# A seven-product feed-forward projection over ten of sixteen chunks of K instead of eight

## The chip, the cores and the metric

The kernel runs on one core of one Trainium2 chip. The metric is the device time of one execution in microseconds; before the change it is 1642.07 us, the median of three runs (1641.97 to 1642.49). All data are float32.

## What is computed

Two transformer blocks run one behind the other on 256 tokens of width 2048: a mixer block (attention, short convolution, pooling, output projection, layer norm), and a block of gated linear attention, a SwiGLU feed-forward part, a gate with an embedding and a last norm. The change touches the feed-forward part alone:

```python
def swiglu(hn, w_in, w_out):            # hn (256, 2048), w_in (2048, 11264), w_out (5632, 2048)
    gate, up = jnp.split(jnp.einsum('btd,de->bte', hn, w_in), 2, axis=-1)
    return jnp.einsum('btf,fd->btd', jax.nn.silu(gate) * up, w_out)
```

## The kernel before

**Products in split float32.** Every float32 operand is split in two: a rounded high part (`hi`, type float32r, by a ScalarE copy) and the rest (`lo = x - hi`, by a VectorE subtraction). A product is then three matmuls: hi x hi, hi x lo, lo x hi. So a block of weights with K rows in chunks of 128 costs one ScalarE copy, one VectorE subtraction and three matmuls for each chunk and each of the two tiles of 128 tokens.

**The feed-forward loop.** The inner width 5632 is cut into `NF = 11` steps of 512 columns. In step f the kernel computes the 512 gate and the 512 up columns (K = 2048, 16 chunks), and the part of the output product that belongs to step f-1 (`o0` to `o3`, four blocks of 4 chunks by 512 columns, each for both token tiles).

**Seven products for eight.** Chunks 8 to 15 are multiplied plainly: `g0` and `g1` (gate), `u0` and `u1` (up), four chunks each for both token tiles, 24 matmuls a block. Chunks 0 to 7 are taken as a two-by-two block product in the Strassen-Winograd form. The blocks on the one side are the token tile (first or second 128) by the half of the chunks (0 to 3 or 4 to 7); on the other side the half of the chunks by gate or up (`w11`, `w12`, `w21`, `w22`). Eight block products become seven, `f11 f21 f22 ft1 ft2 ft3 ft4`, each for one token tile of sums, 12 matmuls. The sums on the side of the weights are made in each step by VectorE in place (`block_sum`, line 2157, four a step), those on the side of the activations once (`form_sums`, `s_hi`, `s_lo`). VectorE combines the seven results (`combine`, line 2164, eight 128x512 operations a step).

**The order of the work.** It is written out by hand, and each engine takes its own list in order. On TensorE a step is

`g0 f11 g1 (turn) f21 u0 ft1 o0 f22 u1 ft2 o1 ft3 o2 ft4 o3`

where `turn` transposes the activations of step f-1 (line 1066). ScalarE makes the `hi` of the same blocks in the same order (lines 1499 and 1511), with `copy_p1` (1518, which takes the result of `f11` out of the accumulator), the `silu` calls (1525) and `split_act` (1585, of the transposed activations, between `ft1` and `o0`) among them. VectorE makes the `lo` (2144) in the same order; between the `lo` of `ft1` and of `o0` stand the low half of `split_act` (2275, two operations) and one `block_sum`.

**Buffers.** There are `SPLITS = 3` pairs of `hi` and `lo` buffers used in turn, so the `hi` of a block waits until TensorE is done with the block three places before it. There are `RAWS = 6` buffers for raw weights. SyncE issues the loads (line 576) in order, each as soon as the `lo` that used the buffer last is done: `w11` and `w21` follow the `lo` of `ft4` of the step before, `g1` the `lo` of `o3`.

**The first and the last step.** The first step (`FIRST`) has no output blocks and takes `g0 u0 f11 g1 ft1 f21 f22 ft2 ft3 ft4 u1`. The last (`LAST`) takes `ft3 ft4 o1 o2 o3` at its end. Ahead of the first stands the last panel of the projection before, which reads its operand from `y_hi` and `y_lo`.

Of the kernel before, what the change touches and what calls it, by code (L numbers as in the profile page):

```python
# [76 lines left out]
RAWS, SPLITS = 6, 3  # L77
FORMS = 7
# [26 lines left out]
(L_X, L_Y, L_Z, L_22A, L_22, L_21, L_11, L_12) = range(1, COMBOS + 1)  # L105
EARLY_0 = 6
# [149 lines left out]
def block_kernel(nc, x, x_cols, w_in, fg_cols, b_f, columns, pool_cols, w_out, ln_g, ln_b, p_cols,  # L256
# [7 lines left out]
    def at(name, shape, dt, offset):  # L264
# [73 lines left out]
    s_sum = [at(f"s_sum{k}", [P, QUAD, P], F32, W + (40 + 2 * k) * KB) for k in range(4)]
    s_hi = [at(f"s_hi{k}", [P, QUAD, P], F32R, s_at[k]) for k in range(FORMS)]
    s_lo = [at(f"s_lo{k}", [P, QUAD, P], F32R, s_at[FORMS + k]) for k in range(FORMS)]  # L340
    up = [at(f"up{t}", [P, N], F32, (108 + 2 * t) * KB) for t in range(TT)]
    act_tok = at("act_tok", [P, TT, N], F32, 80 * KB)
    act_hi = at("act_hi", [P, N // P, TOK], F32R, 84 * KB)
    act_lo = at("act_lo", [P, N // P, TOK], F32R, 88 * KB)
# [58 lines left out]
    with ExitStack() as ctx:  # L403
# [109 lines left out]
        def s_sources():  # L513
# [3 lines left out]
            return ((F11, h_cols[:, 0:QUAD, one]), (F21, h_cols[:, QUAD:, one]), (FT4, h_cols[:, QUAD:, two]),  # L517
# [8 lines left out]
        def _(sp):  # L526
# [35 lines left out]
            def quad_rows(w, r, col):  # L562

                return w[r:r + QUAD * P, col:col + N].rearrange("(c p) n -> p c n", p=P)

            def load_quad(key, src):

                slot, count, freed = RAW[key]
                place = (slot + 2) % RAWS
                if freed is not None:  # L570
                    sp.wait_ge(d_lo_done, freed + 1)
                elif place < 2:
                    sp.wait_ge(lo_done, U_END - RING + 2 * (place + 1))
                else:
                    sp.wait_ge(unit_used, U_END - RING + 2 * (place % 2 + 1))
                sp.dma_start(d_raw[slot][:], src).then_inc(d_landed[slot], 16)

            def load_in(name, f, row, col):

                load_quad((name, f), quad_rows(ffn_w_in[0], row * QUAD * P, col * D_FF + f * N))  # L580

            def load_out(name, f, n):

                load_quad((name, f), quad_rows(ffn_w_out[0], (f - 1) * N, n * N))

            load_in("g0", 0, 2, 0)
            load_in("u0", 0, 2, 1)
            load_in("w11", 0, 0, 0)
            load_in("w12", 0, 0, 1)
            load_in("g1", 0, 3, 0)  # L590
            load_in("w22", 0, 1, 1)
            load_in("w21", 0, 1, 0)
            load_in("u1", 0, 3, 1)
            for f in range(1, NF):
                load_in("g0", f, 2, 0)
                load_in("w11", f, 0, 0)
                load_in("w21", f, 1, 0)
                load_in("g1", f, 3, 0)
                load_in("w12", f, 0, 1)
                load_in("u0", f, 2, 1)  # L600
                load_in("w22", f, 1, 1)
                load_out("o0", f, 0)
                load_in("u1", f, 3, 1)
# [123 lines left out]
        def _(pe):  # L727
# [305 lines left out]
            def quad_tile(e, bank, hi, lo, k, t, st, en):  # L1033

                tok = slice(t * P, (t + 1) * P)
                for c in range(QUAD):
# [3 lines left out]
                    mm = pe.matmul(bank[:], lo[:, k + c, tok], wh, start=False, stop=en and c == QUAD - 1)  # L1040
# [4 lines left out]
            def quad(e, banks, hi, lo, k, st, en, i=0):  # L1045

                pe.wait_ge(d_lo_done, i * E_STEP + (e + 1))
                for t in range(TT):
                    mm = quad_tile(e, banks[t], hi, lo, k, t, st, t in en)
# [25 lines left out]
            quad(FIRST["g0"], gate_banks, a_hi, a_lo, 2 * QUAD, True, NONE)  # L1075
# [4 lines left out]
            quad(FIRST["u0"], up_banks, a_hi, a_lo, 2 * QUAD, True, NONE)  # L1080
# [3 lines left out]
            quad(FIRST["g1"], gate_banks, a_hi, a_lo, 3 * QUAD, False, NONE)  # L1084
# [7 lines left out]
            quad(FIRST["u1"], up_banks, a_hi, a_lo, 3 * QUAD, False, BOTH)  # L1092
# [10 lines left out]
            def ffn_step(at, f, i=0, first=False, last=False):  # L1103

                pe.wait_ge(combined, EARLY_0 if first else i * COMBOS + COMBOS * f)
                quad(at["g0"], gate_banks, a_hi, a_lo, 2 * QUAD, True, NONE, i)
# [12 lines left out]
                quad(at["u1"], up_banks, a_hi, a_lo, 3 * QUAD, False, BOTH, i)  # L1119
# [71 lines left out]
        def _(act):  # L1191
# [301 lines left out]
            def high_of(e, raw, i=0):  # L1493
# [5 lines left out]
                nc.scalar.copy(d_hi[e % SPLITS][:], d_raw[slot][:]).then_inc(d_hi_done, 1)  # L1499

            def quad_high(at, name, f, i=0):

                high_of(at[name], (FORM_RAW.get(name, name), f), i)
# [24 lines left out]
            def split_h(name, n, col):  # L1528
                for i in (2 * n, 2 * n + 1):
                    split_high(name, i, a_hi, 2 * i, h1_hi_done if name == "h1" else h2_hi_done, col + 2 * i)  # L1530

            def columns_of(i, bank, done):

                for k in range(2):
                    c = 2 * i + k
                    last = nc.scalar.activation(h_cols[:, c, :], bank[:, k * TOK:(k + 1) * TOK], ACT.Copy,
                                                scale=vec[:, V_FFN + c:V_FFN + c + 1])
                last.then_inc(done, 1)

            for n in range(PO):  # L1540
                for j in range(UPP):
# [7 lines left out]
                    if n >= 1 and j == 1:  # L1549
                        if n == PO - 1:  # L1550
                            split_h("h1", n - 1, V_FFN)
                        else:
                            for i in (2 * n - 2, 2 * n - 1):
                                job_done(act, "h1", i)
                                columns_of(i, bank_of("h1", i), read_of("h1", i))
                        squares(1, n - 1)
                    if (n, j) == (2, 4):
                        act.wait_ge(s_summed, 4)
                        for k, src in s_sources():
                            nc.scalar.copy(s_hi[k][:], src).then_inc(s_hi_done, 1)  # L1560
# [26 lines left out]
            def ffn_step(at, f, i=0, last=False):  # L1587
# [76 lines left out]
        def _(dve):  # L1664
# [471 lines left out]
            def split_h(name, n, col):  # L2136
                for i in (2 * n, 2 * n + 1):
                    done, count = (h1_hi_done, 2 * (i - 3)) if name == "h1" else (h2_hi_done, 2 * (i + 1))
                    split_low(name, i, a_hi, a_lo, 2 * i, done, count, col + 2 * i)

            def low_of(e, slot, i=0):

                dve.wait_ge(d_hi_done, i * E_STEP + (e + 1))
                nc.vector.tensor_tensor(d_lo[e % SPLITS][:], d_raw[slot][:], d_hi[e % SPLITS][:],  # L2144
                                        ALU.subtract).then_inc(d_lo_done, 1)

            def quad_low(at, name, f, i=0):

                low_of(at[name], RAW[(FORM_RAW.get(name, name), f)][0], i)
# [275 lines left out]
```

## Time and profile before

| | |
|---|---|
| median of three runs | 1642.07 us |
| the profiled execution | 1642.43 us |
| its span, first to last instruction | 1640.7 us |
| TensorE busy | 1625.9 us, 99% |
| VectorE busy | 1224.6 us, 75% |
| ScalarE busy | 852.5 us, 52% |
| mean granted TensorE clock | 0.998 |
| DMA | 316.00 MB, 193 GB/s |

The feed-forward steps lie between 838 and 1519 us of the span. A matmul's record is longer than its share of the engine, since matmuls overlap: the distance from one start to the next is what it costs. The same holds in a smaller measure for VectorE and ScalarE, where the next instruction starts up to 0.1 us before the end of the record in front of it.

### The profile page before, as it was taken

How to read it: one execution, taken by the hardware profiler on the slowest of the kernel's cores; microseconds unless marked ns; L12 is line 12 of the kernel's file. 1: busy time of each engine (PE TensorE's matmuls, PEld its weight loads, DVE VectorE, ACT ScalarE, POOL GpSimd, SP SyncE). 2: the span in 40 equal slices, each digit the busy share in tenths (PEclk: the TensorE clock that was granted, in tenths of full speed). 3: DMA queues.
4: the chain of work that ended last, by engine and by line, in shares of the span. 5: the costliest groups of instructions: out<-in, count | busy, mean ns of one | idle time of the engine just before them, and what ended most of it. 6: DMA issues, size and time to landing. Idle time of an engine off the chain costs nothing.

```text
span 1640.7 us, 21707 instructions
## 1 busy us (share of the span) xinstructions
PE 1625.9 (99%) x8508; PEld 1337.3 (82%) x8508; DVE 1224.6 (75%) x1168; ACT 852.5 (52%) x880; POOL 57.1 (3%) x83
## 2 busy tenths in 40 slices
PE   9999999999999999999999999999999999999997
PEld 7888888888888888888887888888888888887886
DVE  5544476566787999765679988988888888889754
ACT  5435454444568565665555545454545554554543
POOL 7000000000010000000000000000000000000001
PEclk9999999999999999999999999999999999999999
DMA  8666655766575656635575546456467376365841
GB/s 278 174 186 184 189 162 160 232 226 211 164 246 165 187 173 180 181 116 189 163 250 205 185 174 242 164 207 231 138 221 255 109 249 226 132 230 213 299 154 52
DMA packets 156776, 316.00 MB, mean 193 GB/s; under 512 B 7360, under 2 KB 7360, under 8 KB 155808
## 3 DMA queue, kind: packets, MB, share of 16 engines
q1 hardware_dynamic: 155088, 304.12, 56.8%
q0 software_dynamic: 1616, 10.87, 1.8%
q8 instruction: 51, 0.84, 0.2%
q14 instruction: 21, 0.17, 0.0%
HBM read 310.77 MB, written 4.19 MB: 192 GB/s over the span
## 4 chain that ended last, share of the span: by engine, by line
PE 96%; DVE 2%; issue 1%; ACT 1%; POOLq 0%; POOL 0%; DVEq 0%; ACTq 0%
PE acc L739 15%; PE acc L741 15%; PE acc L740 15%; PE acc L1038 9%; PE acc L1039 9%; PE acc L1040 9%; PE aux L1038 7%; PE aux L1040 6%; PE aux L1039 6%; DVE d_lo L2144 1%; PE aux L755 1%; PE aux L925 1%; PE aux L767 1%; PE acc L1066 0%; PE aux L776 0%
## 5 line engine op out<-in xcount | busy, mean ns | idle before, releaser
L2144 DVE TENSOR_TENSOR d_lo<-d_raw,d_hi 128x2048 fp32r<-128x2048 f32 x181 | 413.8, 2287 | 117.2 <-ACT d_hi L1499 83.9
L1676 DVE TENSOR_TENSOR w_lo<-w_raw,w_hi 128x1024 fp32r<-128x1024 f32 x276 | 336.1, 1224 | 204.7 <-ACT w_hi L1198 203.9
L1198 ACT CAST w_hi<-w_raw 128x1024 fp32r<-128x1024 f32 x276 | 289.2, 1049 | 338.9 <-PE acc L741 309.9
L1499 ACT CAST d_hi<-d_raw 128x2048 fp32r<-128x2048 f32 x137 | 262.2, 1914 | 226.0 <-PE acc L1040 126.1
L739 PE MATMUL acc<-w_hi,a_hi 128*128 128x512 f32 x832 | 330.4, 397 | 0.0
L741 PE MATMUL acc<-w_hi,a_lo 128*128 128x512 f32 x832 | 324.2, 390 | 0.0
L740 PE MATMUL acc<-w_lo,a_hi 128*128 128x512 f32 x832 | 324.1, 390 | 0.0
L741 PEld LDWEIGHTS acc<-w_hi,a_lo 128*128 128x128 f32 x832 | 156.2, 188 | 33.1
L739 PEld LDWEIGHTS acc<-w_hi,a_hi 128*128 128x128 f32 x832 | 156.2, 188 | 32.0 <-issue 0.3
L740 PEld LDWEIGHTS acc<-w_lo,a_hi 128*128 128x128 f32 x832 | 156.4, 188 | 30.6
L1511 ACT CAST d_hi<-d_raw 128x2048 fp32r<-128x2048 f32 x44 | 84.2, 1914 | 116.6 <-PE aux L1040 67.5
L1038 PE MATMUL aux<-d_hi,a_hi 128*128 128x512 f32 x352 | 137.1, 390 | 0.7 <-DVE d_lo L2144 0.7
L1040 PE MATMUL aux<-d_hi,a_lo 128*128 128x512 f32 x352 | 136.9, 389 | 0.0
L1039 PE MATMUL aux<-d_lo,a_hi 128*128 128x512 f32 x352 | 136.9, 389 | 0.0
L1038 PE MATMUL acc<-d_hi,act_hi 128*128 128x512 f32 x320 | 124.8, 390 | 1.5 <-DVE act_tok L2191 1.5
L1040 PE MATMUL acc<-d_hi,act_lo 128*128 128x512 f32 x320 | 124.5, 389 | 0.0
L1039 PE MATMUL acc<-d_lo,act_hi 128*128 128x512 f32 x320 | 124.5, 389 | 0.0
L2157 DVE TENSOR_TENSOR d_raw<-d_raw,d_raw 128x2048 f32<-128x2048 f32 x44 | 100.4, 2283 | 1.0 <-DMA d_raw<-in_ffn_w_in 1.0
L739 PE MATMUL acc<-w_hi,y_hi 128*128 128x512 f32 x256 | 100.1, 391 | 0.0
L741 PE MATMUL acc<-w_hi,y_lo 128*128 128x512 f32 x256 | 99.7, 389 | 0.0
L740 PE MATMUL acc<-w_lo,y_hi 128*128 128x512 f32 x256 | 99.6, 389 | 0.0
L1038 PEld LDWEIGHTS aux<-d_hi,a_hi 128*128 128x128 f32 x352 | 66.1, 188 | 14.7 <-DVE d_lo L2144 1.1
(312 smaller groups left out, 2208.7 us busy)
## 6 DMA issues: line engine op xcount, KB each, us to landing
d_raw<-in_ffn_w_in SPq DMA_DIRECT2D x88, 1024.0 KB, 7.3
w_raw<-in_w_in SPq DMA_DIRECT2D x112, 512.0 KB, 3.7
w_raw<-in_gla_w_in SPq DMA_DIRECT2D x96, 512.0 KB, 3.8
d_raw<-in_ffn_w_out SPq DMA_DIRECT2D x44, 1024.0 KB, 5.1
w_raw<-in_w_out SPq DMA_DIRECT2D x32, 512.0 KB, 4.7
w_raw<-in_gla_w_out SPq DMA_DIRECT2D x32, 512.0 KB, 3.8
d_raw<-in_ple_w_gate SPq DMA_DIRECT2D x16, 1024.0 KB, 5.2
x_raw<-in_x_cols SPq DMA_DIRECT2D x8, 256.0 KB, 6.7
```

The source lines that it names most:

```text
L739: pe.matmul(banks[t][:], hi[:, k + c, tok], wh, start=st, stop=False)
L740: pe.matmul(banks[t][:], hi[:, k + c, tok], wl, start=False, stop=False)
L741: mm = pe.matmul(banks[t][:], lo[:, k + c, tok], wh, start=False, stop=en)
L1038: pe.matmul(bank[:], hi[:, k + c, tok], wh, start=st and c == 0, stop=False)
L1039: pe.matmul(bank[:], hi[:, k + c, tok], wl, start=False, stop=False)
L1040: mm = pe.matmul(bank[:], lo[:, k + c, tok], wh, start=False, stop=en and c == QUAD - 1)
L1198: nc.scalar.copy(w_hi[u % RING][:], w_raw[u % RING][:]).then_inc(hi_done, 1)
L1499: nc.scalar.copy(d_hi[e % SPLITS][:], d_raw[slot][:]).then_inc(d_hi_done, 1)
L1511: nc.scalar.copy(d_hi[e % SPLITS][:], d_raw[slot][:]).then_inc(d_hi_done, 1)
L1676: nc.vector.tensor_tensor(w_lo[u % RING][:], w_raw[u % RING][:], w_hi[u % RING][:], ALU.subtract).then_inc(lo_done, 1)
L2144: nc.vector.tensor_tensor(d_lo[e % SPLITS][:], d_raw[slot][:], d_hi[e % SPLITS][:], ALU.subtract).then_inc(d_lo_done, 1)
L2157: nc.vector.tensor_tensor(x[:], x[:], d_raw[SLOT[other]][:], ALU.add).then_inc(d_summed, 1)
```

## The change

The block products take ten chunks (`HALF = 5`, so two halves of five) and the plain blocks six: `g0` and `u0` have two chunks, `g1` and `u1` four. The output blocks keep four. With larger blocks the memory is laid out anew: the third pair of splits takes the place of `y_hi` and `y_lo`, so the first `f11` waits for the end of the panel before; `p1` and `cx` have no tiles of their own and lie in `act_tok`, `cy` lies in `up[1]`. `copy_p1` therefore waits until the old `act_tok` is turned, and stands behind the `hi` of `u0`. The split of the activation sums moves from the third to the fourth panel of the projection before. The loads of the end take the raw buffers in another order.

```diff
+HALF = 5
+PLAIN = (2, 4)
-(L_X, L_Y, L_Z, L_22A, L_22, L_21, L_11, L_12) = range(1, COMBOS + 1)
-EARLY_0 = 6
+(L_X, L_Y, L_12, L_Z, L_22A, L_22, L_21, L_11) = range(1, COMBOS + 1)
+EARLY_0 = 5
+def chunks_of(name):
+    if name in ("g0", "u0", "g1", "u1"):
+        return PLAIN[int(name[1])]
+    return HALF if name[0] in "fw" else QUAD
...
-        place(("fe", n), (1, 3, 0, 2)[n], E_FE + n)
+        place(("fe", n), (1, 3, 2, 4)[n], E_FE + n)
-        place(("pg", q), (4, 5, 1, 3, 0, 2)[q % RAWS], E_PG + q)
+        place(("pg", q), (5, 1, 3, 2, 4)[q % 5], E_PG + q)
...
-    d_raw = [at(f"d_raw{r}", [P, QUAD, N], F32, 8 * ((r + 2) % RAWS) * KB) for r in range(RAWS)]
-    d_hi = [at(f"d_hi{r}", [P, QUAD, N], F32R, W + 8 * r * KB) for r in range(SPLITS)]
-    d_lo = [at(f"d_lo{r}", [P, QUAD, N], F32R, W + (24 + 8 * r) * KB) for r in range(SPLITS)]
+    raw_at = [60 * KB, 16 * KB, 26 * KB, 36 * KB, 0, 8 * KB]
+    d_raw = [at(f"d_raw{r}", [P, HALF if r < 4 else QUAD, N], F32, raw_at[r]) for r in range(RAWS)]
+    d_hi = [at(f"d_hi{r}", [P, HALF, N], F32R, (W + 10 * r * KB, 80 * KB)[r == 2]) for r in range(SPLITS)]
+    d_lo = [at(f"d_lo{r}", [P, HALF, N], F32R, (W + (20 + 10 * r) * KB, 90 * KB)[r == 2]) for r in range(SPLITS)]
...
-    p1 = at("p1", [P, N], F32, W + 60 * KB)
-    cx = at("cx", [P, N], F32, W + 62 * KB)
-    cy = at("cy", [P, N], F32, W + 64 * KB)
+    p1, cx, cy = act_tok[:, 0, :], act_tok[:, 1, :], up[1]
...
-            quad(FIRST["g0"], gate_banks, a_hi, a_lo, 2 * QUAD, True, NONE)
+            quad(FIRST["g0"], gate_banks, g_hi, g_lo, 0, True, NONE, n=PLAIN[0])
...
-                mm = quad_tile(e, bank, s_hi[k], s_lo[k], 0, 0, st, en)
+                mm = quad_tile(e, bank, s_hi[k], s_lo[k], 0, 0, st, en, HALF)
...
-                nc.scalar.copy(d_hi[e % SPLITS][:], d_raw[slot][:]).then_inc(d_hi_done, 1)
+                nc.scalar.copy(d_hi[e % SPLITS][:, 0:n, :], d_raw[slot][:, 0:n, :]).then_inc(d_hi_done, 1)
...
                 act.wait_ge(d_used, i * E_STEP + (at["f11"] + 1))
                 if f:
-                    act.wait_ge(combined, i * COMBOS + (COMBOS * (f - 1) + C_11))
-                nc.scalar.copy(p1[:], acc[2][:]).then_inc(p1_read, 1)
+                    act.wait_ge(act_turned, i * TT + TT * f)
+                nc.scalar.copy(p1, acc[2][:]).then_inc(p1_read, 1)
...
-                    if (n, j) == (2, 4):
+                    if (n, j) == (3, 3):
                         act.wait_ge(s_summed, 4)
...
+            act.wait_ge(unit_used, U_END)
             act.wait_ge(s_lo_done, FORMS)
             quad_high(FIRST, "f11", 0)
...
                 quad_high(at, "g1", f, i)
                 quad_high(at, "f21", f, i)
+                quad_high(at, "u0", f, i)
                 copy_p1(at, f, i)
-                quad_high(at, "u0", f, i)
                 sum_high(at, "ft1", f, i)
                 split_act(f - 1, act_hi, acc[0:2], i)
...
                     quad_low(at, "o1", f)
-                    combine(cx[:], acc[0], cx[:], ALU.add, at["ft3"], f, 0, L_Y)
+                    combine(up[0][:], aux[2], cy[:], ALU.add, at["u1"], f, 0, L_Y)
+                    combine(cx, acc[0], cx, ALU.add, at["ft3"], f, 0, L_X)
...
                     combine(act_tok[:, 0, :], aux[0], p1[:], ALU.add, at["f21"], f)
-                    combine(up[0][:], aux[2], cy[:], ALU.add, at["u1"], f, 0, L_Y)
                     multiply(1, f)
```

## Rows read from the trace of the kernel before

**Rows 1.** The page, busy time: engine, us, share of span, instructions.
```profile
PE 1625.9 (99%) x8508; PEld 1337.3 (82%) x8508; DVE 1224.6 (75%) x1168; ACT 852.5 (52%) x880; POOL 57.1 (3%) x83
```
**Rows 2.** Waits of TensorE: released by, us in total, times, longest us.
```profile
PE acc L1038 <- DVE act_tok L2191: 1.5, 1, 1.5
...
PE acc L1038 <- DVE d_lo L2144: 0.8, 1, 0.8
PE aux L1038 <- DVE d_lo L2144: 0.7, 1, 0.7
```
**Rows 3.** Busy time by stretch: PE, PEld, DVE, ACT, POOL, clock, DMA share, GB/s.
```profile
1200.00:1260.00 60.00, 60.00 (x278) 49.49 (x277) 52.45 (x38) 30.46 (x20) 0.00 (x0) 1.00 0.54 185
1500.00:1560.00 60.00, 58.50 (x287) 48.11 (x286) 45.97 (x53) 32.41 (x46) 1.84 (x3) 1.00 0.85 316
1631.00:1641.00 10.00, 0.31 (x2) 0.00 (x0) 3.36 (x7) 2.56 (x4) 0.55 (x1) 0.70 0.55 210
```
**Rows 4.** Timeline of TensorE, one middle step: start, duration, first matmuls of blocks.
```profile
1021.69 0.39 PE L1040 MATMUL aux<-d_hi,a_lo 128*128 128x512 f32 x1
1022.01 0.71 PE L1066 MATMUL acc<-ident,act_tok 64*128 64x64 f32 x16
1022.66 0.50 PE L1038 MATMUL aux<-d_hi,s_hi 128*128 128x512 f32 x1
...
1025.53 0.39 PE L1038 MATMUL aux<-d_hi,a_hi 128*128 128x512 f32 x1
...
1030.97 0.39 PE L1038 MATMUL acc<-d_hi,s_hi 128*128 128x512 f32 x1
...
1033.69 0.39 PE L1038 MATMUL acc<-d_hi,act_hi 128*128 128x512 f32 x1
```
**Rows 5.** Timeline of ScalarE, same step.
```profile
1008.52 1.91 ACT L1499 CAST d_hi<-d_raw 128x2048 fp32r<-128x2048 f32 x1 [2.54 <-PE acc L1040]
...
1016.75 0.59 ACT L1518 COPY p<-acc 128x512 f32<-128x512 f32 x1 [0.88 <-PE acc L1040]
1017.24 1.91 ACT L1499 CAST d_hi<-d_raw 128x2048 fp32r<-128x2048 f32 x1
1022.12 1.91 ACT L1511 CAST d_hi<-d_raw 128x2048 fp32r<-128x2048 f32 x1 [2.97 <-PE aux L1040]
```
**Rows 6.** Timeline of VectorE, same step.
```profile
1024.06 2.29 DVE L2144 TENSOR_TENSOR d_lo<-d_raw,d_hi 128x2048 fp32r<-128x2048 f32 x1 [1.47 <-ACT d_hi L1511]
1026.27 1.28 DVE L2275 TENSOR_TENSOR act_lo<-acc,act_hi 128x512 fp32r<-128x512 f32 x2
1027.47 2.28 DVE L2157 TENSOR_TENSOR d_raw<-d_raw,d_raw 128x2048 f32<-128x2048 f32 x1
1029.67 2.29 DVE L2144 TENSOR_TENSOR d_lo<-d_raw,d_hi 128x2048 fp32r<-128x2048 f32 x1
```
**Rows 7.** The page's groups: VectorE and ScalarE instructions of two and four chunks.
```profile
L2144 DVE TENSOR_TENSOR d_lo<-d_raw,d_hi 128x2048 fp32r<-128x2048 f32 x181 | 413.8, 2287 | 117.2 <-ACT d_hi L1499 83.9
L1676 DVE TENSOR_TENSOR w_lo<-w_raw,w_hi 128x1024 fp32r<-128x1024 f32 x276 | 336.1, 1224 | 204.7 <-ACT w_hi L1198 203.9
L1198 ACT CAST w_hi<-w_raw 128x1024 fp32r<-128x1024 f32 x276 | 289.2, 1049 | 338.9 <-PE acc L741 309.9
L1499 ACT CAST d_hi<-d_raw 128x2048 fp32r<-128x2048 f32 x137 | 262.2, 1914 | 226.0 <-PE acc L1040 126.1
```
**Rows 8.** Timeline of SyncE's DMA issues, same step.
```profile
996.47 0.92 SPq L576 DMA_DIRECT2D d_raw<-in_ffn_w_in  x2
...
1000.59 0.92 SPq L576 DMA_DIRECT2D d_raw<-in_ffn_w_in  x2
```
**Rows 9.** The tile of raw weights, window 1000 to 1002: `g1` and `w12`.
```profile
DMA to landing us min/median/max: 7.5/9.4/11.4
```
**Rows 10.** Timeline of TensorE: first matmuls of `g0` and `u1`, first step.
```profile
837.75 0.39 PE L1038 MATMUL aux<-d_hi,a_hi 128*128 128x512 f32 x1
...
875.87 0.50 PE L1038 MATMUL aux<-d_hi,a_hi 128*128 128x512 f32 x1 [0.66 <-DVE d_lo L2144]
```

More of the change, by code:

```diff
@@ L338, in block_kernel @@
[L338 to L344, printed above, removed]
@@ new lines, in block_kernel @@
+    s_hi = [at(f"s_hi{k}", [P, HALF, P], F32R, s_at[k]) for k in range(FORMS)]
+    s_lo = [at(f"s_lo{k}", [P, HALF, P], F32R, s_at[FORMS + k]) for k in range(FORMS)]
+    g_hi = at("g_hi", [P, KD - 2 * HALF, TOK], F32R, 48 * KB)
+    g_lo = at("g_lo", [P, KD - 2 * HALF, TOK], F32R, 54 * KB)
+    up = [at("up0", [P, N], F32, W + 67 * KB), at("up1", [P, N], F32, 46 * KB)]
+    act_tok = at("act_tok", [P, TT, N], F32, 100 * KB)
+    act_hi = at("act_hi", [P, N // P, TOK], F32R, 104 * KB)
+    act_lo = at("act_lo", [P, N // P, TOK], F32R, 108 * KB)
@@ L516, in s_sources @@
             one, two = slice(0, P), slice(P, TOK)
-            return ((F11, h_cols[:, 0:QUAD, one]), (F21, h_cols[:, QUAD:, one]), (FT4, h_cols[:, QUAD:, two]),
+            return ((F11, h_cols[0][:, :, one]), (F21, h_cols[1][:, :, one]), (FT4, h_cols[1][:, :, two]),
                     (FT1, s_sum[0][:]), (FT3, s_sum[2][:]), (FT2, s_sum[1][:]), (F22, s_sum[3][:]))
@@ L582, in load_out @@
-            def load_out(name, f, n):
[L584 to L593, printed above, removed]
-            for f in range(1, NF):
[L595 to L601, printed above, removed]
+                else:
+                    sp.wait_ge(*after)
@@ new lines, in _ @@
+            load_in("g0", 0, (lo_done, U_END - RING + 2))
+            load_in("u0", 0, (lo_done, U_END))
+            load_in("w11", 0, (unit_used, U_GO))
+            load_in("w12", 0, (unit_used, U_END - 1))
+            load_in("g1", 0)
+            load_in("w22", 0, (unit_used, U_END))
+            load_in("w21", 0, (unit_used, U_END))
+            load_in("u1", 0)
+            for f in range(1, NF):
+                load_in("g0", f)
+                load_in("w11", f)
+                load_in("w21", f)
+                load_in("g1", f)
+                load_in("w12", f)
+                load_in("u0", f)
+                load_in("w22", f)
@@ L1031, in _, with quad_tile @@
                         turn_h("h1", 2 * n - 1)
-            def quad_tile(e, bank, hi, lo, k, t, st, en):
+            def quad_tile(e, bank, hi, lo, k, t, st, en, n=QUAD):
                 tok = slice(t * P, (t + 1) * P)
-                for c in range(QUAD):
+                for c in range(n):
                     wh, wl = d_hi[e % SPLITS][:, c, :], d_lo[e % SPLITS][:, c, :]
@@ L1039, in quad_tile, with quad @@
                     pe.matmul(bank[:], hi[:, k + c, tok], wl, start=False, stop=False)
-                    mm = pe.matmul(bank[:], lo[:, k + c, tok], wh, start=False, stop=en and c == QUAD - 1)
+                    mm = pe.matmul(bank[:], lo[:, k + c, tok], wh, start=False, stop=en and c == n - 1)
                 return mm
             BOTH, NONE = range(TT), ()
-            def quad(e, banks, hi, lo, k, st, en, i=0):
+            def quad(e, banks, hi, lo, k, st, en, i=0, n=QUAD):
                 pe.wait_ge(d_lo_done, i * E_STEP + (e + 1))
                 for t in range(TT):
-                    mm = quad_tile(e, banks[t], hi, lo, k, t, st, t in en)
+                    mm = quad_tile(e, banks[t], hi, lo, k, t, st, t in en, n)
                 mm.then_inc(d_used, 1)
@@ L1491, in _, with high_of @@
                         stage_panel(P_G + p, og[p - 8], rstd[1], ACT.Silu)
[L1493 removed]
+            def high_of(e, raw, i=0, n=QUAD):
                 slot, count, _ = RAW[raw]
@@ L1529, in split_h, with columns_of, plain_columns @@
                 for i in (2 * n, 2 * n + 1):
[L1530 to L1532 removed]
+                    split_high(name, i, a_hi, 2 * i, h2_hi_done, col + 2 * i)
+            def columns_of(i):
+                job_done(act, "h1", i)
                 for k in range(2):
                     c = 2 * i + k
[L1536 to L1538 removed]
+                    last = nc.scalar.activation(h_cols[c // HALF][:, c % HALF, :], bank_of("h1", i)[:, k * TOK:(k + 1) * TOK],
+                                                ACT.Copy, scale=vec[:, V_FFN + c:V_FFN + c + 1])
+                last.then_inc(read_of("h1", i), 1)
+            def plain_columns():
+                i = HALF
+                job_done(act, "h1", i)
+                for k in range(2):
+                    c = 2 * i + k
+                    nc.scalar.activation(g_hi[:, k, :], bank_of("h1", i)[:, k * TOK:(k + 1) * TOK], ACT.Copy,
+                                         scale=vec[:, V_FFN + c:V_FFN + c + 1]).then_inc(h1_hi_done, 1)
             for n in range(PO):
@@ L1566, in _ @@
                     col = 2 * (2 * PO - 2 + k) + c
-                    last = nc.scalar.activation(a_hi[:, col, :], acc[k][:, c * TOK:(c + 1) * TOK], ACT.Copy,
+                    last = nc.scalar.activation(g_hi[:, col - 2 * HALF, :], acc[k][:, c * TOK:(c + 1) * TOK], ACT.Copy,
                                                 scale=vec[:, V_FFN + col:V_FFN + col + 1])
@@ L2168, in combine_xy @@
                 dve.wait_ge(p1_read, i + (f + 1))
-                combine(cx[:], acc[2], p1[:], ALU.subtract, at["ft2"], f, i)
-                combine(cy[:], acc[3], cx[:], ALU.add, at["ft1"], f, i, C_X)
+                combine(cx, acc[2], p1, ALU.subtract, at["ft2"], f, i)
+                combine(cy[:], acc[3], cx, ALU.add, at["ft1"], f, i, C_X)
             def combine_one(at, f, i=0):
                 dve.wait_ge(act_turned, i * TT + TT * f)
-                combine(act_tok[:, 0, :], aux[0], p1[:], ALU.add, at["f21"], f, i)
+                combine(act_tok[:, 0, :], aux[0], p1, ALU.add, at["f21"], f, i)
                 combine(up[0][:], aux[2], cy[:], ALU.add, at["u1"], f, i, C_Y)
             def combine_late(at, f, i=0):
-                combine(cx[:], acc[2], cx[:], ALU.add, at["ft3"], f, i, C_Y)
+                combine(cx, acc[2], cx, ALU.add, at["ft3"], f, i, C_Y)
                 combine(up[1][:], acc[2], cy[:], ALU.add, at["ft3"], f, i)
@@ L2195, in split_h @@
                 for i in (2 * n, 2 * n + 1):
-                    done, count = (h1_hi_done, 2 * (i - 3)) if name == "h1" else (h2_hi_done, 2 * (i + 1))
-                    split_low(name, i, a_hi, a_lo, 2 * i, done, count, col + 2 * i)
+                    split_low(name, i, a_hi, a_lo, 2 * i, h2_hi_done, 2 * (i + 1), col + 2 * i)
             def form_sums():
                 one, two = slice(0, P), slice(P, TOK)
-                a11, a12 = h_cols[:, 0:QUAD, one], h_cols[:, QUAD:, one]
-                a21, a22 = h_cols[:, 0:QUAD, two], h_cols[:, QUAD:, two]
-                for i in range(4):
+                a11, a12 = h_cols[0][:, :, one], h_cols[1][:, :, one]
+                a21, a22 = h_cols[0][:, :, two], h_cols[1][:, :, two]
+                for i in range(HALF):
                     job_read(dve, "h1", i)
@@ L2257, in _ @@
             dve.wait_ge(p1_read, 1)
-            combine(cx[:], acc[2], p1[:], ALU.subtract, FIRST["ft2"], 0)
-            combine(cy[:], acc[3], cx[:], ALU.add, FIRST["ft1"], 0, 0, C_X)
-            combine(act_tok[:, 0, :], aux[0], p1[:], ALU.add, FIRST["f21"], 0)
+            combine(cx, acc[2], p1, ALU.subtract, FIRST["ft2"], 0)
+            combine(cy[:], acc[3], cx, ALU.add, FIRST["ft1"], 0, 0, C_X)
+            combine(act_tok[:, 0, :], aux[0], p1, ALU.add, FIRST["f21"], 0)
             quad_low(FIRST, "u1", 0)
-            combine(cx[:], acc[0], cx[:], ALU.add, FIRST["ft3"], 0, 0, 3)
-            combine(up[1][:], acc[0], cy[:], ALU.add, FIRST["ft3"], 0)
+            combine(cx, acc[0], cx, ALU.add, FIRST["ft3"], 0, 0, 3)
             def combine_first_up():
                 combine(up[0][:], aux[2], cy[:], ALU.add, FIRST["u1"], 0)
-                combine(up[1][:], aux[3], up[1][:], ALU.add, FIRST["u1"], 0, 0, 5)
-                dve.wait_ge(combined, 7)
+                combine(up[1][:], acc[0], cy[:], ALU.add, FIRST["ft3"], 0)
+                combine(up[1][:], aux[3], up[1][:], ALU.add, FIRST["u1"], 0, 0, 7)
                 multiply(0, 0)
```

91 lines of the change are left out of this document (44 added, 47 removed).

## The prediction

> **What bounds the kernel now.** I read the busy times first: TensorE 99% of the span, VectorE 75%, ScalarE 52% [rows 1]. The whole kernel waits on TensorE's list. The waits of TensorE say the same: in the eleven feed-forward steps there are three, 1.5, 0.8 and 0.7 us [rows 2], two in the first step and one in the last. The stretches then show how near the next engine is: in 60 us of the middle steps TensorE is busy for 60.0 and VectorE for 52.45 [rows 3]. So a step has some 7.5 us of VectorE's time to spare in 60. That is an average. What decides is each place where a block's `lo` must be ready, and the places differ, so I looked at one step by engine [rows 4 to 6].
>
> **What a step costs each engine.** Twelve matmuls of `ft1` take from 1030.97 to 1033.69, so one costs 2.72 / 12 = 0.2267 us [rows 4]. Before, a step has 4 x 24 (plain) + 7 x 12 (products) + 4 x 24 (output) = 276. After: `g0` and `u0` 12 each, `g1` and `u1` 24 each, 7 x 15, 96: 273. TensorE saves 3 x 0.2267 = 0.68 us a step, 7.5 us in eleven steps. That is all that the change can gain.
>
> VectorE pays for it. Two chunks take 1224 ns and four 2287, so a chunk is 0.53 us and a five-chunk subtraction 2.82 (estimate by the straight line of these two rows) [rows 7]; the block sums are 2.28 and so 2.81 [rows 6]. A step gets 7 + 4 chunks more and 4 fewer: 7 x 0.53 = 3.7 us more on an engine that had some 7.5 to spare. ScalarE: 1049 and 1914 ns give 0.43 a chunk and 2.35 for five [rows 7]; it gets 3 chunks more, 1.3 us, and has half its time free. On the average both still fit under TensorE. The bytes of a step are the same: 16 chunks for gate, 16 for up, 16 for the outputs.
>
> **The place where it does not fit: `o0` in every step.** In the order of the work `u0` stands between the turn and `o0`, and it is one of the blocks that shrink. Before, from the last matmul of `g1` the chain is: `hi` of `ft1` at 1022.12, as soon as `g1` has left its buffers; `lo` of `ft1` at 1024.06; two `act_lo` at 1026.27; a block sum at 1027.47; `lo` of `o0` 1029.67 to 1031.96 [rows 5, 6]. TensorE comes to `o0` at 1033.69 [rows 4], so 1.73 us are left over.
>
> After, counted from the same `g1`:
> - TensorE. The turn and `f21` take from 1021.92 (0.23 behind 1021.69) to 1025.53 with 12 matmuls [rows 4]; with 15 `f21` ends at 1026.21. `u0` with 12 takes 2.72, to 1028.93; `ft1` with 15 takes 3.40, to 1032.33. `o0` is due 1.36 us earlier than before.
> - ScalarE. `copy_p1` stood at 1016.75 in the shadow of `g1` [rows 5]. It now writes into `act_tok`, so it waits for the end of the turn, 1022.01 + 0.71 = 1022.72, and what is queued behind it is the `hi` of `ft1`, `split_act`, `o0`. A waiting engine starts 0.04 after its releaser (1022.08 to 1022.12 [rows 4, 5]): 1022.76. The next instruction starts 0.49 later (1016.75 to 1017.24 [rows 5]): `hi` of `ft1` at 1023.25, 1.13 later than before, and ready at 1025.60.
> - VectorE. `lo` of `ft1` starts at 1025.63 and holds the engine for 2.21 + 0.53 = 2.74 (to 1028.37); `act_lo` 1.20 (1029.57); the block sum 2.20 + 0.53 = 2.73 (1032.30); `lo` of `o0` 2.29, ready at 1034.59 [steps from rows 6, 7].
>
> So data are 2.63 us later (1.13 by the wait for the turn, 0.43 and twice 0.53 by fifth chunks) and the need is 1.36 earlier; the 1.73 to spare turn into a stall of 2.30 with 0.04 for the release. The first matmul after a stop is 0.11 longer (0.50 against 0.39 [rows 10, 4]). A step: 2.30 + 0.11 - 0.68 = 1.73 us slower. No row shows a five-chunk instruction. From below, were the fifth chunk free (2.29 and 1.91), the data would come 1.49 earlier: a stall of 0.8, a step 0.25 slower. From above, in proportion with the fixed part (2.287 x 1.25 = 2.86, 1.914 x 1.25 = 2.39), 0.12 later: 1.85. The straight line through two and four chunks is the nearest, so I take 1.73.
>
> **`g1` and its load.** `w11` and `w21` are issued when the `lo` of `ft4` is done, 996.47, `g1` at 1000.59 [rows 8]; `g1` landed 7.5 us later [rows 9], so 11.6 after the first, with 3 MB in the queue. The queue moves up to 316 GB/s [rows 3], 3.3 us for 1 MB. In front of `g1` now stand 2.5 MB instead of 2: 13.25 us. ScalarE could start it at 1008.52 [rows 5], 12.05 after the issue; I take 12.45 after the change, as `ft4` is longer on TensorE. It waits 0.8. TensorE comes to `g1` 2.72 + 3.40 = 6.12 after that point, and `hi` 1.91, `lo` 2.2 and the multiply 0.74 (with the releases) need 4.95. So 0.35 is left. Landings of neighbouring loads scatter by about 1 us (7.5 and 11.4 for two issued together [rows 9]); I allow 0.2 a step, 1.8 for nine steps.
>
> **The first step.** It has no output blocks, so its 7 products and 4 sums crowd VectorE, which already stopped TensorE for 0.8 and 0.7 [rows 2]. The `hi` of `f11` now waits for the end of the panel, just past 837.75 [rows 10]: 837.95. Then `hi` to 840.30; VectorE: `lo` of `f11` to 843.07, sum to 845.80, the last columns of h (1.6) to 847.4, `lo` of `g1` to 849.6, a root (0.45) to 850.05, nine five-chunk instructions (5 `lo` and 3 sums up to `ft3`, and `ft4`) of 2.735 to 874.7, three combinations of 0.6 to 876.5, `lo` of `u1` (2.29) to 878.8. With some 0.3 of waits between, `u1` starts on TensorE at 879.1 against 875.87 [rows 10]: 3.2 slower. The moved split of the sums lies in the fourth panel, on VectorE and ScalarE, which have waits there; it ends about 2 us before `g0` is due: nothing.
>
> **The second step.** `ft4`'s `lo` ends near 874.8 and with it the loads start: `g1` lands at 888.1, is split at 892.3 and multiplied at 893.0; TensorE is there at 879.1 + 5.44 + 2.72 + 3.40 = 890.7. A stall of 2.3 and 0.1 for the start, and the 1.73 of `o0`: 4.1 slower.
>
> **The last step.** Its `o0` stalls like the others, +1.73. The stop of 1.5 at `o2` [rows 2] shrinks: one combination (0.6) has moved ahead of the `lo` of `o2`, and TensorE comes later. I take 0.7 off: +1.0. Behind it the raw buffers are five instead of six; a block of the end is 24 matmuls, 5.44 us, against 3.3 to load 1 MB: nothing. If that cover fell, each of 20 blocks could lose up to a microsecond.
>
> **Sum.** 3.2 + 4.1 + 8 x 1.73 + 1.0 + 1.8 = 23.9 us. The profiled execution took 1642.4 (span 1640.7 and 1.7 around it), 0.4 above the median of the runs: 1642.4 + 23.9 = 1666.3. As a second stall at `ft1` or `f22` costs more than a saved one gives back, I round up to 1667.
>
> **Rivals.**
> - *The loads decide.* For: `g1` has 0.35 us left, and 1.25 MB loads are longer. Against: bytes and the share of DMA time, 0.54 [rows 3], are unchanged. At 3.6 us for 1 MB `g1` lands 1.05 later; 0.7 to 1.1 a step, ten steps, 7 to 11 more: 1674 to 1678.
> - *TensorE stays the bound (the other side).* The stall at `o0` does not come, because VectorE and ScalarE run through that chain in the time that they have on the average. Then 11 x 0.68 = 7.5 less: 1635. For: 7.5 us to spare on VectorE in 60 against 3.7 [rows 3]. Against: the order of the lists; VectorE is idle while ScalarE waits for the turn and can't work ahead. It decides from a chain 1.7 us shorter, where stall and saving are equal.
> - *TensorE's clock falls.* The granted clock is 1.00 in the stretch with the stop of 1.5 us and 0.70 in the last 10 us, where TensorE is busy for 0.31 [rows 3]: between 1.2 and 2.4 GHz, 0.70 is 6 of 10 us at the lower. If each of some 14 stops of 2.3 us brought 3 us at half speed, 1.5 each: 21 more, 1688. The Trainium skill, page "TensorE: Matmul & The Clock Gate", section "HAM oscillation — how this bites in real kernels", says that waits repeated in a loop can make the clock fall and rise in each round. By that rule this rival holds; for it speaks that stops come in every step, against it that each is short and 57 us of dense work follow.
>
> **Chances.** The sum as worked out, 0.78 (1655 to 1672); loads 0.13; clock 0.04; faster 0.05. Times within 0.2% (3.3 us), about what a measurement of this kernel can tell from no change, need the stall near 0.7: I give 0.02, taken from the first and the faster case, so faster 0.04, slower 0.94. The range 1657 to 1679 leaves out the faster and the clock case and the ends of the others.
>
> **What would show it.** The waits of TensorE after: one group at `acc` released by `d_lo`, about ten times of 2.3 us, at `o0`; in ScalarE's row of the `p` copy a releaser of line 1066's turn; five-chunk rows 128x2560 of 2.8 us on VectorE and 2.35 on ScalarE. A wait at `g1` of 2 to 3 us in the second step alone. Step length 65.2; before it is 276 x 0.2267 and 0.89 for the turn (1021.92 to 1025.53 less 2.72) [rows 4], 63.5. Wrong, if the waits of TensorE are under 7 us in all, if they stand at other blocks than `o0`, or if the clock is below 0.99.

## The result, and the profile after

The changed kernel takes 1670.61 us (median of six runs, 1669.84 to 1671.34) against 1642.28 for the kernel before in the same session: 1.0172 times as long, interval 1.0159 to 1.0185. The profiled execution has a span of 1669.6 us, 28.9 more than before.

The waits of TensorE, all of them (what it waited for, us in total, times, longest):

```profile
PE acc L1049 <- DVE d_lo L2164: 23.3, 11, 2.3
PE aux L1049 <- DVE d_lo L2164: 4.1, 3, 2.1
PE aux L1049 <- DVE act_tok L2211: 2.5, 1, 2.5
PE aux L787 <- DVE still L1721: 1.3, 1, 1.3
PE acc L1049 <- DVE act_tok L2211: 0.9, 1, 0.9
PE acc L797 <- ACT w_hi L1209: 0.7, 1, 0.7
PE aux L992 <- ACT lr_flat L1416: 0.3, 1, 0.3
```

The first line is the forecast one: ten times 2.2 to 2.35 us at `o0`, and 1.1 once in the first step. Before, that group had one wait of 0.8 [rows 2]. In the timeline of TensorE each of the ten stands at the first matmul of `o0`. One middle step, from the last matmuls of `g1` to `o0`:

```profile
1163.58 0.39 PE L1051 MATMUL aux<-d_hi,g_lo 128*128 128x512 f32 x1
1163.90 0.71 PE L1077 MATMUL acc<-ident,act_tok 64*128 64x64 f32 x16
1164.55 0.50 PE L1049 MATMUL aux<-d_hi,s_hi 128*128 128x512 f32 x1
...
1168.10 0.39 PE L1049 MATMUL aux<-d_hi,g_hi 128*128 128x512 f32 x1
...
1170.82 0.39 PE L1049 MATMUL acc<-d_hi,s_hi 128*128 128x512 f32 x1
...
1176.55 0.50 PE L1049 MATMUL acc<-d_hi,act_hi 128*128 128x512 f32 x1 [2.17 <-DVE d_lo L2164]
```

`f21` takes until 1168.10, `u0` until 1170.82 (2.72, where it had 5.44 before), `ft1` 3.40. ScalarE and VectorE in the same stretch:

```profile
1164.68 0.59 ACT L1529 COPY act_tok<-acc 128x512 f32<-128x512 f32 x1 [5.06 <-PE acc L1077]
1165.16 2.34 ACT L1522 CAST d_hi<-d_raw 128x2560 fp32r<-128x2560 f32 x1
```
```profile
1167.54 2.82 DVE L2164 TENSOR_TENSOR d_lo<-d_raw,d_hi 128x2560 fp32r<-128x2560 f32 x1 [3.29 <-ACT d_hi L1522]
1170.28 1.28 DVE L2292 TENSOR_TENSOR act_lo<-acc,act_hi 128x512 fp32r<-128x512 f32 x2
1171.48 2.82 DVE L2177 TENSOR_TENSOR d_raw<-d_raw,d_raw 128x2560 f32<-128x2560 f32 x1
1174.21 5.02 DVE L2164 TENSOR_TENSOR d_lo<-d_raw,d_hi 128x2048 fp32r<-128x2048 f32 x2
```

The releaser of the copy is the matmul at line 1077, the turn (the copy is `copy_p1`, whose target `p1` is now the first half of `act_tok`); behind it stands the `hi` of `ft1`, and VectorE is idle for 3.29 us before it gets the `lo` of `ft1`. From there it runs without a gap to `o0`, whose `lo` starts at 1174.21 and ends 2.29 later. The five-chunk instructions take 2.82 and 2.34. Against [rows 4 to 6] everything from the turn to `o0` has the forecast lengths.

The second thing to see is the clock. Busy time by stretch (PE, PEld, DVE, ACT, POOL, granted clock, DMA share, GB/s), the first row right behind the stop at `o0` of the second step, the other 60 us of the middle steps:

```profile
912.40:916.00 3.60, 3.60 (x9) 2.89 (x10) 3.60 (x2) 0.00 (x0) 0.00 (x0) 0.54 0.69 241
1200.00:1260.00 60.00, 57.80 (x267) 47.32 (x266) 53.37 (x35) 30.28 (x19) 0.00 (x0) 1.00 0.55 193
```

And the first four matmuls of that stretch:

```profile
912.40 0.50 PE L1049 MATMUL acc<-d_hi,act_hi 128*128 128x512 f32 x1 [2.32 <-DVE d_lo L2164]
912.71 0.62 PE L1050 MATMUL acc<-d_lo,act_hi 128*128 128x512 f32 x1
913.13 0.63 PE L1051 MATMUL acc<-d_hi,act_lo 128*128 128x512 f32 x1
913.56 0.63 PE L1049 MATMUL acc<-d_hi,act_hi 128*128 128x512 f32 x1
```

They start 0.427 us apart instead of 0.227, with a granted clock of 0.54 in the row: the lower level, 1.2 GHz instead of 2.4, right after TensorE had stood still for 2.32 us. Such rows are found in four places, 7, 8, 7 and 8 matmuls, so 30 x 0.20 = 6.0 us are lost to the clock. The steps of the trace show it as two lengths: from one `o0` to the next 65.2 to 65.4 us (six times) or 66.84 to 66.86 (three times). By these lengths a stretch costs 1.6 us, so the four cost up to 6.4.

### The profile page after: what moved, and what is told of

Same layout as the page of the kernel before. It is cut to its first block, busy times and chain, and to the rows that moved or that the text cites. A ratio compares the mean times of both kernels' runs of the same rounds, so it can differ in the third digit from the quotient of the medians.

```text
span 1669.6 us, 21621 instructions
## 1 busy us (share of the span) xinstructions
PE 1627.2 (97%) x8475; PEld 1334.6 (80%) x8475; DVE 1267.0 (76%) x1166; ACT 865.0 (52%) x880; POOL 56.4 (3%) x83
## 4 chain that ended last, share of the span: by engine, by line
PE 85%; DVE 6%; issue 4%; ACT 2%; DMA 2%; DVEq 0%; ACTq 0%; POOLq 0%; POOL 0%; SPq 0%
PE acc L750 15%; PE acc L752 14%; PE acc L751 14%; PE acc L1049 8%; PE acc L1051 8%; PE acc L1050 8%; PE aux L1049 4%; PE aux L1050 4%; PE aux L1051 4%; DVE d_lo L2164 3%; ACT d_hi L1522 2%; DVE d_raw L2177 1%; DMA d_raw<-in_ffn_w_in 1%; PE aux L766 1%; DMA w_raw<-in_gla_w_in 1%
## 5 line engine op out<-in xcount | busy, mean ns | idle before, releaser
L2164 DVE TENSOR_TENSOR d_lo<-d_raw,d_hi 128x2560 fp32r<-128x2560 f32 (+2 forms) x181 | 430.7, 2386 | 108.1 <-ACT d_hi L1510 63.1
L1510 ACT CAST d_hi<-d_raw 128x2048 fp32r<-128x2048 f32 (+2 forms) x137 | 257.2, 1881 | 198.1 <-PE acc L1051 143.0
L1522 ACT CAST d_hi<-d_raw 128x2560 fp32r<-128x2560 f32 x44 | 103.2, 2345 | 117.1 <-PE acc L1051 74.9
L2177 DVE TENSOR_TENSOR d_raw<-d_raw,d_raw 128x2560 f32<-128x2560 f32 x44 | 124.0, 2818 | 0.0
L1049 PE MATMUL aux<-d_hi,g_hi 128*128 128x512 f32 x264 | 103.9, 394 | 4.6 <-DVE act_tok L2211 2.5
L1050 PE MATMUL aux<-d_lo,g_hi 128*128 128x512 f32 x264 | 103.2, 391 | 0.0
L1051 PE MATMUL aux<-d_hi,g_lo 128*128 128x512 f32 x264 | 103.2, 391 | 0.0
L1049 PEld LDWEIGHTS acc<-d_hi,act_hi 128*128 128x128 f32 x320 | 61.3, 191 | 40.3 <-DVE d_lo L2164 20.9
```

The lines of the kernel that those rows point to most:

```text
L1049: pe.matmul(bank[:], hi[:, k + c, tok], wh, start=st and c == 0, stop=False)
L1050: pe.matmul(bank[:], hi[:, k + c, tok], wl, start=False, stop=False)
L1510: nc.scalar.copy(d_hi[e % SPLITS][:, 0:n, :], d_raw[slot][:, 0:n, :]).then_inc(d_hi_done, 1)
L2164: nc.vector.tensor_tensor(d_lo[e % SPLITS][:, 0:n, :], d_raw[slot][:, 0:n, :], d_hi[e % SPLITS][:, 0:n, :], ALU.subtract).then_inc(d_lo_do ...
L2177: nc.vector.tensor_tensor(x[:], x[:], d_raw[SLOT[other]][:], ALU.add).then_inc(d_summed, 1)
```

## The experiments

Two theories. *A, a chain with a place:* the loss is the chain turn, copy, `ft1`, `act_lo`, sum, `o0`, and each stop costs its length and now and then a stretch at the lower clock. *B, throughput:* VectorE's 3.7 us more a step fill it up, wherever the order puts them. A third, the loads, came in for the second step. The changed kernel itself was not timed again beside the experiments; the kernel before was, and its medians stayed between 1642.38 and 1642.84.

**The clock alone: matmuls of no use in the stops.**

```diff
                 pe.wait_ge(act_lo_done, i * TT + TT * f)
+                for _ in range(10):
+                    pe.matmul(acc[0][:], s_hi[0][:, 0, :], g_hi[:, 0:2, :], start=True, stop=True)
                 out_panel(at["o0"], acc[0:2], i)
```

(written out here without its helper; ten more stand ahead of `g1` in the second step). In the expectation of this run A and B are two theories of the clock alone, not the two above.

> Kernel after, with ten matmuls of no use (into a bank that is overwritten next) issued ahead of o0 in each step, where TensorE stands still for 2.2 us, and ten ahead of g1 in the second step. No data arrive earlier. Theory A (the stops let the clock fall; 30 matmuls of the trace after stand 0.43 us apart instead of 0.23, four stretches, 6 us in all): the steps keep their 65.2 us, the long ones of 66.8 vanish, granted clock over 0.998, 5 to 6 us faster than after, about 1665. Theory B (the stops cost only their own length and the 66.8 us steps have another cause): 1670 to 1671 as after. Slower than after by 2 us or more would say that the filling is late itself.

1664.96 us, 5.65 less than after; 1.014 times before (1.0123 to 1.0157), granted clock 0.998. No matmul of the feed-forward steps stands at the lower clock, and the waits at `o0` are gone from the list, since the filling takes their time. The data come no earlier: the middle steps stay 65.2 to 65.4 us long. So of 28.3 us of loss some 5.7 are the clock's, in agreement with 30 x 0.20 within the scatter of the four runs (1663.76 to 1666.49).

**The copy behind `ft1`.**

```diff
-                copy_p1(at, f, i)
                 sum_high(at, "ft1", f, i)
+                copy_p1(at, f, i)
```

> Kernel after, with copy_p1 behind the hi of ft1 on ScalarE instead of ahead of it; no other change. Theory A (the chain from the turn to o0 is the bound: 1.13 of its 2.63 us is the wait of copy_p1 for the turn): hi of ft1 starts 1.13 us earlier, the stop at o0 falls from 2.2 to 1.1 in ten steps, 11 to 12 us faster than after, and 2 to 6 us more if the clock no longer falls: 1653 to 1660. Rival (VectorE's total work of a step is the bound, 3.7 us more of it than before): moving a copy on ScalarE changes nothing, 1669 to 1672, and the stop moves to a later block.

1653.94 us (1.0071, 1.0055 to 1.0088). The first three waits of TensorE in the list:

```profile
PE acc L1049 <- DVE d_lo L2164: 11.6, 11, 1.2
PE aux L1049 <- DVE act_tok L2211: 2.4, 1, 2.4
PE aux L1049 <- DVE d_lo L2164: 2.1, 1, 2.1
```

Each stop fell from 2.2 to 1.0, as the 1.13 of the copy's wait asks. Steps are 64.1 us, and none of the stops of 1.0 is followed by a stretch at the lower clock. B would have left them as they were.

**The sum behind `o0`.**

```diff
                 split_act(f - 1, act_hi, act_lo, acc[0:2], i)
-                block_sum("w11", "w22", f, i)
                 quad_low(at, "o0", f, i)
+                block_sum("w11", "w22", f, i)
```

> Kernel after, with the block sum for ft2 behind the lo of o0 on VectorE instead of ahead of it; VectorE's work is the same in sum. Theory A: 2.73 us leave the chain to o0, so its stop of 2.2 goes, but the blocks behind are later by as much and the next stop comes at u1: about 1.3 us there and 0.2 at g1; a step of 64.4 instead of 65.2: 8 us faster, and 3 to 6 more by the clock: 1656 to 1663. Rival (throughput of VectorE): total 1669 to 1672 with the stop at u1 as long as it was at o0. Second rival (only the one place): no stop left at all, steps of 62.8, 1640 to 1645.

1654.63 us (1.0072, 1.0055 to 1.0089), 1.4 below the expected range. The first three waits:

```profile
PE aux L1049 <- DVE d_lo L2164: 14.3, 13, 2.1
PE aux L1049 <- DVE act_tok L2211: 2.5, 1, 2.5
PE acc L1049 <- DVE d_lo L2164: 1.4, 2, 1.1
```

The group changed from `acc` to `aux`: the stop is at `u1` now, 1.0 us, and not at `o0`. A middle step is 64.1 us. That is 0.3 better than expected (1.0 at `u1`, not 1.3, and nothing at `g1`). Neither B's unchanged total nor the cure without remainder came.

**The wait in the kernel before.** `copy_p1` moved behind the `hi` of `u0` and made to wait for the turn, blocks of four.

```diff
-                copy_p1(at, f, i)
                 quad_high(at, "u0", f, i)
+                copy_p1(at, f, i)
...
-                    act.wait_ge(combined, i * COMBOS + (COMBOS * (f - 1) + C_11))
+                    act.wait_ge(act_turned, i * TT + TT * f)
```

> Kernel before, with copy_p1 behind the hi of u0 and waiting for the turn, as in after; blocks of four chunks stay. Theory A: the chain to o0 gets 1.13 us longer, of 1.73 to spare: 0.6 left, no new stop of TensorE, 1642 to 1643. If the wait by itself makes the loss: stops at o0 of a microsecond or more, 1652 or slower.

1642.39 against 1642.38 (1.0001, 0.9991 to 1.001). The waits of TensorE in the feed-forward steps are those of [rows 2]. ScalarE's copy now waits for the turn there too (to 1022.13 in the step of [rows 5]). So a longer chain cost nothing while 1.73 us were to spare; in the changed kernel the same wait costs some eleven us over ten steps.

**Four chunks in the new layout.**

```diff
-HALF = 5
-PLAIN = (2, 4)
+HALF = 4
+PLAIN = (4, 4)
```

(with the addresses and the split of the h columns that go with it, and a wait of the first `hi` of `g0` and `u0` for the `lo` of the sums)

> Kernel after with blocks of four chunks again (HALF = 4, plain blocks of four and four), but with everything else of the change: the new places in memory, p1 and cx in act_tok, the copy's wait for the turn, the raw buffers of the end, the later split of the sums; the hi of g0 and u0 of the first step wait for the lo of the sums, since they would overwrite them. Theory A (the loss comes from five-chunk blocks and the shorter u0 in the chain to o0): steps of 63.45 us and no stop at o0, the first step at most 2 us later; 1642 to 1645. If the layout or the waits that came with it make the loss: 1655 or more.

1643.15 us (1.0002, 0.9993 to 1.0011). No wait at `o0` is left. The layout, the shared tiles, the later split and the five raw buffers of the end cost nothing that can be told. The number of chunks makes the loss: it lengthens the blocks of the chain and shortens the `u0` that covered it, and this run takes both back at once.

**Both moves together.**

> Kernel after, with copy_p1 behind the hi of ft1 and the block sum for ft2 behind the lo of o0 (the two single moves gave 1653.9 and 1654.6). Theory A (a chain with a place: both take time out of the chain to o0, and what is left over moves to u1): the 1.0 us stop at o0 and the 1.0 at u1 both go, about 0.1 left at u1 and 0.2 at g1, steps of 63.2 us; 1645 to 1648. Were the two moves worth the same microsecond (VectorE's throughput behind both), the step would stay at 64.1: 1653 to 1655.

1643.94 us (1.0011, 1.0001 to 1.002): lower than expected by a microsecond, for the steps are 62.97 us long (the same load is issued at 1186.35 and at 1249.32), not 63.2. The two moves gave 16.7 and 16.0 alone and 26.7 together, the 22 us of stops and the clock's share. The middle steps have no wait at all, and TensorE's saving can be seen, 0.5 us a step of the 0.68 worked out. What is left lies in the first two steps and the last.

**The load of `g1` ahead of that of `w21`.**

```diff
-                load_in("w21", f)
                 load_in("g1", f)
+                load_in("w21", f)
```

> Kernel after with the load of g1 ahead of that of w21. Theory A: in the middle steps g1 has enough time already, so nothing changes there (steps of 65.2, stops at o0 of 2.2); in the second step, where TensorE waits 2.5 us at g1 for a load queued behind 2.5 MB, the stop falls to about 0.7: 1.8 us faster, and 1.6 more if no stretch at the lower clock follows: 1667 to 1669. Theory of the loads (they are late in every step): 5 to 10 us faster.

1668.66 us (1.0161, 1.0146 to 1.0177). The number is the expected one, the reason is not. The stop at `g1` of the second step is still there (first two waits of the list):

```profile
PE acc L1049 <- DVE d_lo L2164: 23.2, 11, 2.3
PE aux L1049 <- DVE act_tok L2211: 2.5, 1, 2.5
```

So the load of `g1` was not what it waited for, and the 2 us are not this edit's. The profiled span is 2.8 shorter than after's: 1.2 by the end of the first step, which the edit does not touch and which varies by about a microsecond between the traces, and 1.6 since one stretch at the lower clock fewer lies in the steps behind it. With the two moves as well the same load order changed nothing either:

> Kernel after with the copy behind ft1, the sum behind o0 and the load of g1 ahead of w21. Theory A: steps of 62.9 us, 0.5 shorter than before, against a first step that is 3.3 longer (VectorE is the bound there) and a second with 0.7 us at g1: 1641 to 1644, no change from the kernel before that a measurement can tell. If VectorE's added work costs in other places too: 1646 or more.

1643.69 us (1.0009, 1.0 to 1.0018), 2.3 us of stop at `g1`. ScalarE's timeline of the changed kernel shows the cause:

```profile
879.63 2.34 ACT L1510 CAST d_hi<-d_raw 128x2560 fp32r<-128x2560 f32 x1 [2.13 <-DMA d_raw<-in_ffn_w_in]
886.86 0.72 ACT L1536 ACTIVATE act_tok<-act_tok,rstd 128x512 f32<-128x512 f32 x1 [4.89 <-DVE up L2184]
887.49 5.06 ACT L1510 CAST d_hi<-d_raw 128x2048 fp32r<-128x2048 f32 x3
```

The `hi` of `g1` (887.49) is queued behind a `silu` that waited 4.89 us for a combination into `up`. The `silu` doesn't read `up`; it counts to the eighth combination, and in the first step the last three stand behind the `lo` of `f11`, whose `w11` landed at 879.6.

**The `silu` waits for what it needs.**

```diff
-                silu(1, f - 1, i)
+                silu(1, f - 1, i, ready=(C_11, EARLY_0 if first else C_21))
...
                 quad_low(at, "g1", f, i)
+                if first:
+                    dve.wait_ge(combined, COMBOS)
                 multiply(1, f - 1, i)
```

> Kernel after, where the second silu of the first step waits for the five combinations that it needs and no longer for all eight (VectorE then waits for the eighth ahead of the multiply that reads it). Moving the load of g1 had left the 2.5 us stop at g1 of the second step as it was. Theory C (the hi of g1 stands behind that silu on ScalarE, the silu behind three combinations, these behind the lo of f11 and the end of u1): the hi of g1 starts near 884.7, when u1 leaves its buffers, instead of 887.5; the stop falls from 2.5 to about 0.5: 2 us faster than after and 1.5 more where a stretch at the lower clock goes too, 1666 to 1669. Rival (late loads of the second step): the stop stays at 2.5, 1670 to 1671.

1667.17 us (1.0149, 1.0134 to 1.0165), 3.4 under after. The stop is 0.69 us; of the groups of the feed-forward steps this one fell and no other:

```profile
PE acc L1049 <- DVE d_lo L2164: 23.3, 11, 2.3
PE aux L1049 <- DVE d_lo L2164: 4.1, 3, 2.1
...
PE aux L1049 <- DVE act_tok L2211: 0.7, 1, 0.7
```

The stop itself gave 1.8 us. The rest is clock, and that varies from run to run (granted 0.994 to 0.996): the profiled run has two stretches at the lower clock, where that of after has four, and its span is 4.9 us shorter. What is left of the stop is now the load, as ScalarE's timeline shows for the `hi` of `g1`:

```profile
885.68 4.15 ACT L1510 CAST d_hi<-d_raw 128x2048 fp32r<-128x2048 f32 x2 [3.12 <-DMA d_raw<-in_ffn_w_in]
```

The silu edit was not run together with the other load order.

**All that helped, together:** the two moves, the `silu`, and eight matmuls of no use ahead of `g1` in the first step.

> Kernel after with the copy behind ft1, the sum behind o0 and the earlier silu of the first step, and eight matmuls of no use ahead of g1 in the first step, where TensorE stands still for 2.1 us. Theory: steps of 62.9 us as with the two moves together (1643.9), the stop at g1 of the second step down to 0.5 (2 us), no stretch at the lower clock (1.5 us): 1640 to 1642, at best 0.1% under the kernel before, since the first step stays some 3 us longer. If the remaining stops move elsewhere: 1643 or more.

1641.02 us against 1642.84 in the same session: 0.9988 times before, interval 0.9979 to 0.9997. The middle stretch, to be set against [rows 3]:

```profile
1200.00:1260.00 60.00, 60.00 (x277) 49.17 (x277) 55.57 (x38) 31.95 (x20) 0.00 (x0) 1.00 0.55 191
```

TensorE is back at 60.0 of 60 with VectorE at 55.57 instead of 52.45, and no matmul at the lower clock. The ten-chunk form can so be made to pay a tenth of a percent, an interval that barely leaves out no change. The kernel before has no wait in its middle steps, so the gain there (62.97 us a step against 63.44) is the form's. The silu edit and the filling were not tried on the kernel before, whose waits in the feed-forward steps come to 3.0 us [rows 2].

## Why the prediction was right, and where it was off

The forecast was 1667, the measured 1670.61. Parts of the profiled span, each from the start of one `g0` to the next in TensorE's timeline: first step 837.75 before [rows 10] and 836.09 after; second step, by the start of `f11` less one `g0`, 881.45 and 883.64; first middle step 944.89 and 954.93; last step 1452.39 and 1480.07:

| part | forecast | measured | of it clock |
|---|---|---|---|
| first step | +3.2 | +3.85 | 0 |
| second step | +4.1 | +7.85 | 3.0 |
| eight middle steps | +13.8 | +17.64 | 3.0 |
| last step and end | +1.0 | +1.22 | 0 |
| allowance for late loads | +1.8 | 0 | |
| ahead of the steps | 0 | -1.66 | |
| sum | +23.9 | +28.9 | 6.0 |

- *The stop at `o0`.* Right, place, cause and size: 2.2 us in ten steps (forecast 2.30), 65.24 us a step against 65.2. Its two halves were shown apart: the copy's wait is 1.1 us of it, the sum's place is another part, and with four chunks it isn't there.
- *The average fits, the place doesn't.* Right. The rival by which TensorE stays the bound fell: VectorE's spare time could be used only after the lists were put in another order, and then it could. Even so not without limit: with one of the moves the stop went to `u1`.
- *`g1` and its load.* No wait at `g1` in any middle step, but the working was too pessimistic. ScalarE was to wait 0.8 us for the load in each of them; it waits for no load there, only for TensorE. So about 1.0 us is to spare and not 0.35. In one middle step, whose `g1` starts on TensorE at 1093.13, ScalarE's `hi` of `g1` and VectorE's multiply before it:

```profile
1087.21 1.91 ACT L1510 CAST d_hi<-d_raw 128x2048 fp32r<-128x2048 f32 x1 [2.48 <-PE acc L1051]
```
```profile
1091.36 0.75 DVE L2211 SCALAR_TENSOR_TENSOR act_tok<-up,rstd,act_tok 128x512 f32<-128x512 f32 x1
```

  The 1.8 us of allowance was not needed, and no second stall at `ft1` or `f22`, for which the sum was rounded up, came in the middle steps. The rival of the loads fell, also by the run with the other load order.
- *The second step.* The size was right (2.3, measured 2.5), the cause was wrong, so the size was luck. I let `g1` wait for its own load, landing 13.25 us after the issue of `w11`; by the run with the early `silu` it landed in time for a start at 885.68, 11.85 behind that issue (873.83). It waited behind the `silu` on ScalarE, whose count of combinations I had not followed through the new order.
- *The clock.* This is the term that was missing from the sum. It stood among the rivals as all or nothing, 21 us at a chance of 0.04. It came in part: four stretches of some 1.5 us each: 6.0 by the count of matmuls, 5.7 by the run with the filled stops. The forecast should have given each stop a share of it. That the total still came out within 4 us is also due to the allowance of 1.8 that was not needed and to 1.66 less ahead of the steps. The Trainium skill, page "TensorE: Matmul & The Clock Gate", section "HAM oscillation — how this bites in real kernels", tells of a loop with waits of about 3 to 5 us in which the clock falls again in every round. The traces here agree only in part: the stops were shorter, 2.1 to 2.5 us, and four of the twelve stops over 2 us were followed by a stretch at the lower clock.
- *The first and the last step, layout, end buffers.* Right within 0.7 us. VectorE bounds the first step as worked out; what the sum had too small there is a wait of VectorE of 0.83 us for the `hi` of `ft1` (at 849.10), where 0.3 had been put down. One sign failed: a wait at `g1` was to be seen in the second step alone, and the first has one too, 2.12 us at 848.14, though its working (`lo` of `g1` ready at 849.6) already held it. The layout costs nothing (1643.15). Ahead of the steps nothing was forecast; the stop of 1.1 us for `h_tok` in the kernel before is gone and stops of 0.7 and 0.3 have come, so most of the 1.66 is not explained.

## What to carry to other kernels

Moving work to an engine with spare time on the average is safe only where each consumer still gets its data in time: go through the order of the lists from the last common point to the consumer, add up what is queued, and count also how much shorter the blocks have become that used to cover it. A stop so found can often be taken away by moving one instruction behind the one that is waited for; look then where it comes out next. And follow what a wait counts, not only what the instruction reads.

## What the hardware showed that I had not expected

Stops of 2.1 us and more were at times followed by 7 or 8 matmuls at 1.2 GHz (0.427 us apart), though TensorE had worked without a gap for over 60 us before nine of the fifteen such stretches, and for some 18 us before the other six. Over the feed-forward steps in the profiled runs of seven five-chunk kernels whose stops were left open there were 43 stops of 2.1 us or more and these 15 stretches; behind the 39 stops of 0.5 to 1.8 us there was none. What picks out the 15 of 43 no run here shows. Filling the stops with matmuls of no use gave this time back, 5.7 us of 1670.6, and not that of the stops themselves.
